# A conditioning projection weighed on VectorE and GpSimd instead of multiplied on TensorE, in a two-block fp32 kernel

## What is computed

```python
h = rms_norm(x, pre_ffn_norm)
u = causal_dwconv(h @ w_up, ffn_conv_w, ffn_conv_b)   # 3 taps, 2 x 2816 channels
gate, up = jnp.split(u, 2, axis=-1)
f = (jax.nn.silu(gate) * up) @ w_down
return x + rms_norm(f, post_ffn_norm)
```

```python
def ada_mod(cond, w, b):
    m = jax.nn.silu(cond) @ w + b
    return jnp.split(m, N_MOD, axis=-1)

sh1, sc1, g1, sh2, sc2, g2 = [m[:, None, :] for m in ada_mod(c, w_ada[l], b_ada[l])]
csh1, csc1, cg1, csh2, csc2, cg2 = ada_mod(c_ctx, w_ada[l], b_ada[l])
hc = modulate(rms_norm_2(h_ctx, norm1_g[l]), csh1, csc1)
hx = modulate(rms_norm_2(x, norm1_g[l]), sh1, sc1)
```

## Time and profile before

| | before |
|---|---|
| median of three runs | 1722.95 us |
| profiled execution, its own time | 1724.31 us |
| its span, from the first to the last instruction | 1722.5 us |
| TensorE busy, matmuls | 1638.2 us (95%) |
| TensorE weight loads | 1323.6 us (77%) |
| VectorE busy | 919.8 us (53%) |
| ScalarE busy | 661.0 us (38%) |
| GpSimd busy | 162.8 us (9%) |
| mean granted clock of TensorE | 0.983 |
| DMA | 180.13 MB, mean 105 GB/s |

### The profile page before, as it was taken

How to read it: one execution, slowest core, us unless ns; L and a number is a source line. 1 busy time by engine, 2 the same in 40 slices (tenths; PEclk the granted TensorE clock), 3 DMA queues, 4 the chain that set the end, 5 groups by cost and what they waited for, 6 DMA issues and landing times.

```text
span 1722.5 us, 21472 instructions
## 1 busy us (share of the span) xinstructions
PE 1638.2 (95%) x8319; PEld 1323.6 (77%) x8319; DVE 919.8 (53%) x1383; ACT 661.0 (38%) x1000; POOL 162.8 (9%) x174
## 2 busy tenths in 40 slices
PE   7989989899989899999999999999999799999998
PEld 6777768778868677777788778878777688888886
DVE  5657856774644555545534637865546533333334
ACT  5444465553323433333332532444444322232221
POOL 2011206210000100000000112251000000000000
PEclk9999999999999999999999999999999899999999
DMA  7243324221025366565342322222214133332222
GB/s 197 74 111 86 86 62 111 61 63 49 25 98 193 120 191 217 162 205 166 132 164 97 98 79 61 80 71 67 65 63 130 51 93 94 96 97 98 98 97 73
DMA packets 195687, 180.13 MB, mean 105 GB/s; under 512 B 6014, under 2 KB 175053, under 8 KB 192532
## 3 DMA queue, kind: packets, MB, share of 16 engines
q1 hardware_dynamic: 191888, 169.56, 32.5%
q10 hardware_dynamic: 2564, 8.00, 1.4%
q0 software_dynamic: 1152, 1.44, 0.4%
HBM read 174.63 MB, written 4.58 MB: 104 GB/s over the span
## 4 chain that ended last, share of the span: by engine, by line
PE 67%; DVE 4%; ACT 2%; issue 1%; POOL 0%; POOLq 0%; DVEq 0%; ACTq 0%
PE acc L623 11%; PE acc L624 10%; PE acc L625 10%; PE acc L654 6%; PE acc L656 6%; PE acc L655 6%; PE acc L1130 2%; PE acc L1132 2%; PE acc L1131 2%; PE acc L668 1%; PE acc L667 1%; PE acc L666 1%; PE acc L1077 1%; PE acc L1270 1%; PE acc L1254 1%
## 5 line engine op out<-in xcount | busy, mean ns | idle before, releaser
L1957 DVE TENSOR_TENSOR w_low<-w_raw,w_high 128x1024 fp32r<-128x1024 f32 x230 | 285.2, 1241 | 608.1 <-ACT w_high L1330 607.5
L623 PE MATMUL acc<-h_high,w_high 128*128 128x512 f32 x1216 | 488.0, 401 | 16.1 <-DVE arena L2066 4.9
L1330 ACT ACTIVATE w_high<-w_raw 128x1024 fp32r<-128x1024 f32 x224 | 237.1, 1058 | 633.0 <-PE acc L625 358.9
L624 PE MATMUL acc<-h_low,w_high 128*128 128x512 f32 x1216 | 477.3, 393 | 0.0
L625 PE MATMUL acc<-h_high,w_low 128*128 128x512 f32 x1216 | 477.1, 392 | 0.0
L623 PEld LDWEIGHTS acc<-h_high,w_high 128*128 128x128 f32 x1216 | 231.0, 190 | 94.4 <-issue 29.4
L625 PEld LDWEIGHTS acc<-h_high,w_low 128*128 128x128 f32 x1216 | 230.6, 190 | 49.6
L624 PEld LDWEIGHTS acc<-h_low,w_high 128*128 128x128 f32 x1216 | 230.9, 190 | 46.9 <-issue 1.2
L654 PE MATMUL acc<-w_high,act_high 128*128 128x512 f32 x496 | 194.2, 392 | 4.2 <-DVE arena L2642 1.5
L656 PE MATMUL acc<-w_high,act_low 128*128 128x512 f32 x496 | 193.5, 390 | 0.0
L655 PE MATMUL acc<-w_low,act_high 128*128 128x512 f32 x496 | 193.5, 390 | 0.0
(11 more groups left out here) (372 smaller groups left out, 1923.4 us busy)
## 6 DMA issues: line engine op xcount, KB each, us to landing
w_raw<-w_in SPq DMA_DIRECT2D x68, 512.0 KB, 3.9
w_raw<-w_mlp SPq DMA_DIRECT2D x64, 512.0 KB, 3.7
w_raw<-w_up SPq DMA_DIRECT2D x44, 512.0 KB, 3.9
early<-w_ada SPq DMA_DIRECT2D x22, 1024.0 KB, 6.0
w_raw<-w_out SPq DMA_DIRECT2D x24, 512.0 KB, 3.3
w_raw<-w_down SPq DMA_DIRECT2D x22, 512.0 KB, 3.2
w_raw<-w_branch_gate SPq DMA_DIRECT2D x16, 512.0 KB, 4.1
early<-decay_rows SPq DMA_DIRECT2D x4, 1024.0 KB, 9.6
```

The lines of the kernel that those rows point to most:

```text
L623: pe.matmul(out_, wh, xh, start=start, stop=False)
L624: pe.matmul(out_, wh, xl, start=False, stop=False)
L1330: f(WH[:, off % 2, :], RAW[:, off % 4, :], ACT.Copy).then_inc(sem("w_high"), 1)
L1957: tt(WL[:, off % 2, :], RAW[:, off % 4, :], WH[:, off % 2, :].bitcast(F32), ALU.subtract).then_inc(sem("w_low"), 1)
```

## The change

Only the sum over the 128 partitions stays on TensorE. VectorE multiplies each row of a slab by its conditioning value and adds it to an accumulator of 128 x 2048 (`weighed`, in two halves of 1024 columns, one after the taps of j=0 and one after the products), a slab per q by the table `ADA_DVE`. GpSimd does the same with whole slabs (`weigh_slabs`), a multiplication and an addition each: for slabs 0 to 7 with the context's column (these slabs are weighed by both engines), and for six more by `ADA_POOL`. For each third, `modulation` then multiplies the two accumulators by a column of ones in eight matmuls, after q=10, 14 and 20. The slabs have up to six places, and SyncE asks for slab m behind the weights of the q in `ADA_ASKED`, after whoever used the slab before in that place (`slab_used`). The up-projection alternates between banks 0, 1 and 4, 5, so that a block waits for the taps of four blocks earlier. The loops over q are written out on all engines, and the tile order of `down` follows the banks.

```diff
-SLABS = 24
+ADA_DVE = [[0], [1], [2], [3], [4], [5], [6], [7], [8], [10], [12], [13], [15], [], [], [18], [19], [20], [22], [23]]
+ADA_POOL = [9, 11, 14, 16, 17, 21]
+ADA_PLACE = [m % 4 if m < 18 else [4, 5, 0, 1, 4, 5][m - 18] for m in range(24)]
...
+ADA_ASKED = {1: [0, 1, 2, 3], 4: [4], 5: [5], 6: [6], 7: [7], 8: [8], 9: [9], 10: [10], 11: [11], 12: [12], 13: [13, 14],
+             14: [15], 15: [16, 17], 17: [18, 19], 18: [20], 19: [21, 22], 20: [23]}
...
+        def slab_used(eng, m):
+            if m in ada_order:
+                eng.wait_ge(sem("ada_mult"), 2 * ada_order.index(m) + 2)
+            if m < 8:
+                eng.wait_ge(sem("ada_pool"), m + 1)
+            elif m in ADA_POOL:
+                eng.wait_ge(sem("ada_pool"), 8 + ADA_POOL.index(m) + 1)
+        def ffn_bank(q, j):
+            return 4 * (q % 2) + j
...
-            sp.wait_ge(sem("d_ws"), 2 * NT - 2)
-            for m in range(2):
-                sp.dma_start(first_slab(m), ada_rows[m * P:(m + 1) * P, 0:2048]).then_inc(sem(f"ada_in{m}"), 16)
...
+                if m == 0:
+                    sp.wait_ge(sem("w_used"), UP_N + 2)
+                before = [n for n in range(m) if ADA_PLACE[n] == ADA_PLACE[m]]
+                if before:
+                    slab_used(sp, before[-1])
+                elif m > 3:
+                    sp.wait_ge(sem("mod_sum"), 2)
...
+            def modulation(third):
+                pe.wait_ge(sem("ada_mult"), [16, 26, 36][third])
+                pe.wait_ge(sem("ada_pool"), [8, 11, 14][third])
+                for i, at in enumerate((AD_[third], AG2_[third])):
+                    w = arena(at, 2048).rearrange("p (m g r) -> p m g r", g=4, r=32)
+                    for g in range(4):
+                        o = PS[32 * g:32 * g + 32, [6, 2, 3][third], :].rearrange("p (m r) -> p m r", r=32)
+                        m = pe.matmul(o, CDW[:, i if third == 0 else 0, :], w[:, :, g, :], start=i == 0, stop=i == 1)
+                m.then_inc(sem("mod_sum"), 1)
...
-            modulation(0)
-            modulation(1)
...
-                    pe.wait_ge(sem("ffn_step"), 5 * q + [2, 4][j])
-                    column_block(0, UP_N + 2 * q + j, j, HH, HL)
-                if q < 20:
-                    modulation(q + 2 if q < 11 else q + 3)
-                if q == 10:
-                    modulation(13)
-                if q == 19:
-                    modulation(23)
+                    if q > 1:
+                        pe.wait_ge(sem("ffn_step"), 5 * q - [3, 1][j])
+                    column_block(0, UP_N + 2 * q + j, ffn_bank(q, j), HH, HL)
+                if q in (10, 14, 20):
+                    modulation((10, 14, 20).index(q))
...
-            down(DN_N, DN_A, FF, lambda t, m: turn_x(0, 0) if t == NT - 1 else None, ffn_free, [2, 1, 3, 0])
+            down(DN_N, DN_A, FF, lambda t, m: turn_x(0, 0) if t == NT - 1 else None, ffn_free, [1, 3, 0, 2])
...
+            def weighed(m, part):
+                third, k = m // 8, m % 8
+                i = ada_order.index(m)
+                at = slice(part * 1024, part * 1024 + 1024)
+                acc, w = arena(AD_[third], 2048)[:, at], slab(m)[:, at]
+                slab_in(dve, m)
+                if i == 0 or ada_order[i - 1] // 8 < third:
+                    if third == 2:
+                        dve.wait_ge(sem("mod_sum"), 1)
+                    ts(acc, w, cond[:, k, 0:1], None, ALU.mult).then_inc(sem("ada_mult"), 1)
+                else:
+                    dve.wait_ge(sem("ada_mult"), 2 * i + part - 1)
+                    stt(acc, w, cond[:, k, 0:1], acc, ALU.mult, ALU.add).then_inc(sem("ada_mult"), 1)
...
+            def weigh_slabs():
+                def by(k, who):
+                    return cond[:, k, who:who + 1].to_broadcast([P, 2048])
+                pool.wait_ge(sem("n_low"), 12)
+                for m in [*range(8), *ADA_POOL]:
+                    third, who = m // 8, 1 if m < 8 else 0
+                    acc, w = arena(AG2_[third], 2048), slab(m)
+                    to = arena(M_, 2048) if m < 8 else w
+                    slab_in(pool, m)
+                    if m == 0 or m in (9, 16):
+                        if m == 16:
+                            pool.wait_ge(sem("mod_sum"), 1)
+                        pool.tensor_tensor(acc, w, by(m % 8, who), ALU.mult).then_inc(sem("ada_pool"), 1)
+                        pool.wait_ge(sem("ada_pool"), {0: 1, 9: 9, 16: 12}[m])
+                    else:
+                        step(pool.tensor_tensor(to, w, by(m % 8, who), ALU.mult))
+                        step(pool.tensor_tensor(acc, acc, to, ALU.add))
+                        pool.sem_inc(sem("ada_pool"), 1)
```

More of the change, by code:

```diff
@@ L54 @@
 END_N = M2_N + MF
-SLABS = 24
+ADA_DVE = [[0], [1], [2], [3], [4], [5], [6], [7], [8], [10], [12], [13], [15], [], [], [18], [19], [20], [22], [23]]
+ADA_POOL = [9, 11, 14, 16, 17, 21]
+ADA_PLACE = [m % 4 if m < 18 else [4, 5, 0, 1, 4, 5][m - 18] for m in range(24)]
+ADA_SEM = [place if place < 4 else place - 2 for place in ADA_PLACE]
+ADA_TURN = [sum(ADA_SEM[n] == ADA_SEM[m] for n in range(m)) for m in range(24)]
+ADA_ASKED = {1: [0, 1, 2, 3], 4: [4], 5: [5], 6: [6], 7: [7], 8: [8], 9: [9], 10: [10], 11: [11], 12: [12], 13: [13, 14],
+             14: [15], 15: [16, 17], 17: [18, 19], 18: [20], 19: [21, 22], 20: [23]}
 WO_A, DN_A, W2_A, M2_A = 0, 16, 16 + FF, 24 + FF
@@ L127 @@
 FF_ = 4096
-MR_ = M_
+MR_, MR2_, MRT_, MRT2_ = 15360, M_ + 5632, M_ + 4096, HT_
+AD_, AG2_ = (26624, M_ + 2048, 26624), (16384, M_, 16384)
 GR_, CS_ = 16384, 15360
@@ L348, in blocks, with slab_in @@
                     body(g, j)
-        def up_groups(eng, body):
-            with eng.Fori(0, FF // 8) as cg:
-                for i in range(8):
-                    body(8 * cg + i, i, cg)
-            for i in range(FF % 8):
-                body(FF // 8 * 8 + i, i, FF // 8)
-        def first_slab(m):
-            return arena(K0 * T + m * 2048, 2048)
-        def slab(m):
-            return E[:, (m % 2) * 2048:(m % 2 + 1) * 2048]
+        def slab(m):
+            place = ADA_PLACE[m]
+            if place < 2:
+                return E[:, place * 2048:(place + 1) * 2048]
+            return arena([FF_ + 14 * T, FF_ + 18 * T, XN_, XN_ + 2048][place - 2], 2048)
+        def slab_in(eng, m):
+            eng.wait_ge(sem(f"ada_in{ADA_SEM[m]}"), 16 * (ADA_TURN[m] + 1))
+        ada_order = [m for ms in ADA_DVE for m in ms]
+        def slab_used(eng, m):
[7 more added lines that the diff above has]
+            return 4 * (q % 2) + j
         def probs(u, e):
@@ L573, in _ @@
                     load(0, UP_N + 2 * q + j, w_up_v[:, :, q * P + j * (FF * P):(q + 1) * P + j * (FF * P)], P)
-                if 0 < q < 11:
-                    later_slab(q + 1)
-                if q == 11:
-                    later_slab(12)
-                if q > 10:
-                    later_slab(q + 2)
+                for m in ADA_ASKED.get(q, []):
+                    ask_slab(m)
                 if q == 2:
@@ L1069, in _ @@
             turn_mixed(2)
-            def modulation(m):
-                pe.wait_ge(sem(f"ada_in{m % 2}"), 16 * (m // 2 + 1))
-                w = (first_slab(m) if m < 2 else slab(m)).rearrange("p (m g r) -> p m g r", g=4, r=32)
-                for g in range(4):
-                    o = PS[32 * g:32 * g + 32, [6, 2, 3][m // 8], :].rearrange("p (m r) -> p m r", r=32)
-                    ins = pe.matmul(o, CDW[:, m % 8, :], w[:, :, g, :], start=m % 8 == 0, stop=m % 8 == 7)
-                ins.then_inc(sem("ada_used"), 1)
+            def modulation(third):
[7 more added lines that the diff above has]
+                m.then_inc(sem("mod_sum"), 1)
             pe.wait_ge(sem("cond"), 3)
-            pe.wait_ge(sem("x_res"), NT)
-            modulation(0)
-            modulation(1)
             turn_mixed(NT - 1)
@@ L2440, in ffn @@
                         w = PAR[:, 2, ds(q + (2 - lag) * 2 * FF + j * FF, 1)]
-                        stt(o, PS[:, j, 0:T - lag], w, o, ALU.mult, ALU.add).then_inc(sem("ffn_step"), 1)
+                        stt(o, PS[:, ffn_bank(q, j), 0:T - lag], w, o, ALU.mult, ALU.add).then_inc(sem("ffn_step"), 1)
+                    if j == 0 and q < len(ADA_DVE):
+                        for m in ADA_DVE[q]:
+                            weighed(m, 0)
                 dve.wait_ge(sem("ffn_gate"), q + 1)
@@ L2457, in modulated @@
                 dve.wait_ge(sem("mod_rows"), 2)
-                step(dve.transpose(MRT[:, 32:48, :].rearrange("p a b -> p (a b)"), MR[:, 2, :]))
-                step(tt(modT, MRT[:, :, 0:2], PAR[:, 4, 0:NADA].unsqueeze(2).to_broadcast([P, NADA, 2]), ALU.add))
+                step(dve.transpose(arena(MRT2_, 512), MR2))
+                for t in range(3):
+                    m = tt(modT[:, 16 * t:16 * t + 16, :], MRT[t][:, :, 0:2],
+                           PAR[:, 4, 16 * t:16 * t + 16].unsqueeze(2).to_broadcast([P, 16, 2]), ALU.add)
+                step(m)
```

(4 more changed lines are left out.)

82 lines of the change are left out of this document (45 added, 37 removed).

## The result

| | before | after the change |
|---|---|---|
| median of four runs each, on one chip | 1723.55 us | 1745.79 us (1741.39 to 1751.4) |
| ratio, 95% interval | | 1.0127 (1.0105 to 1.015) |
| profiled execution, its own time | 1724.31 us | 1744.17 us |
| its span | 1722.5 us | 1742.3 us |
| mean granted clock | 0.983 | 0.976 |

A forecast was written before the change was run, and what follows sets the result against it. TensorE was taken to bound the up-projection stage, busy 40.00 of 40.00 us. Terms of -19.5, +42.0 (waits) and +2.5 us (clock) gave +25: 1749 us profiled, 1748 against the median, range 1730 to 1768.

The forecast's parts named there:

- TensorE's part: Up-projection stage: slabs leaving TensorE save 25.7 us, three sums of eight matmuls cost 6.2 us; net -19.5 us.
- VectorE alone fits: Up-projection stage: VectorE's 6.4 us per q plus 2.6 us of weighing, 9.0 of 10.9 us, fits without GpSimd.
- GpSimd's prices: GpSimd's 128x2048 instructions: 3.65 us per multiplication, 4.7 us per addition, all 14 and 11 of them 103 us.
- The exclusion: VectorE and GpSimd instructions that each read two SBUF tensors exclude one another for full length; six such VectorE instructions per q.
- the term for the waits: TensorE in the stage loses 42 us to GpSimd work: 14.4 (slabs 0 to 3), 17.4 (4 to 7), 10.2 (six later).
- the one for the clock: TensorE's lower clock after idling, 1.7 us more per cold block, four or five gaps of 5 us or more: 2.5 us.
- The sign that I named: Profile of the stage: TensorE idle before column blocks, released by w_low, 40 us in sum, most in q=1 to 6.
- Bunched slabs: Slabs 4 to 7: a late VectorE bunches them in pairs of 16.7 us, costing 8.7 us twice, 17.4 us.
- rival 2: Blocking real but mostly absorbed: slabs arriving singly cost 1.9 us each, 32 down to some 20 us; 1723 to 1735; chance 0.06.
- the pause at its start: VectorE's own pause at the start of a run of GpSimd work, some 2 us, subtracted from that run's cost.
- Rival 1: GpSimd's long instructions do not hold VectorE, so only the -19.5 us is left: 1703 us; chance 0.11.
- Rival 3: SyncE stands behind slab_used, weights come late, slabs 4 to 11 cost a further 3 us each: above 1770; chance 0.05.

The follow-up runs named there:

- only writing: Changed kernel with GpSimd's weighing replaced by writing zeros, two 128x2048 instructions for each multiplication and each addition, same waits and counts: 1707.1 us, ratio 0.9903.
- the quiet kernel: Changed kernel with all weighing on GpSimd left out, its accumulators set to zero once and slabs only counted on: 1704.92 us, ratio 0.9882.

## Why the prediction was right

The sign and the mechanism are shown. The stage's lengths by GpSimd's instruction, with VectorE's work the same in all six rows:

| GpSimd's instruction | stage | TensorE idle | split, mean | GpSimd busy |
|---|---|---|---|---|
| 2048 columns | 288.7 us | 26.4 | 2068 ns | 111.2 us |
| 1024 columns | 263.8 | 12.2 | 1795 | 133.2 |
| 512 columns | 258.2 | 7.6 | 1698 | 158.1 |
| 256 columns | 265.5 | 12.4 | 1454 | 192.5 |
| only writing | 248.7 | 0 | 1224 | 91.4 |
| none | 248.3 | 0 | 1224 | 5.4 |

(The last two are those that leave out the weighing.) Point by point:

- **TensorE's part.** Forecast -19.5 us; measured -19.0 us in the stage with GpSimd quiet. The four banks, forecast at nothing, measured 0.9999. The order of the down-projection's tiles gave nothing either.
- **VectorE alone fits.** Forecast 9.0 of 10.9 us per q; the quiet kernel and the one in which VectorE does everything show no idle TensorE.
- **GpSimd's prices.** Multiplication forecast 3.65, measured 3.60 us; addition 4.7, measured 4.60 us. The slope from 512 and 1024 columns carried.
- **The exclusion.** Right, to the 1.07 us between GpSimd's end and the end of VectorE's. "Having passed one GpSimd instruction, VectorE does one of its own and waits for the next" is not exact: a product issued directly behind a short one slips in before GpSimd's next. Five waits per q, not six.
- **The size.** This is where the terms were mis-sized. I forecast 42 us of waits and 2.5 us for the clock, 44.5 in all; measured are 40.4 us, of which 26.4 idle and 14.0 in a TensorE that is busy longer (262.28 against 248.33 us) with the same 1104 matmuls. The clock accounts for most of the 14: by the timeline 70 matmuls of the stage follow each other at the lower level's distance, some 0.2 us too much each, against 15 with GpSimd quiet, which is about 11 us; the first matmuls behind the gaps make up another 1.8 us. "Four or five gaps of 5 us or more" were twelve of 0.3 to 3.4 us, and the lower level followed six of them, of 2.5 to 3.4 us. So the term for the waits was 16 us too high by the idle time, the one for the clock about 8 us too low (2.5 against about 11), and that the sum came within 4 us is in part luck. The two may be tied to each other, since VectorE catches up while TensorE runs slowly, but no run here separates them. The sign that I named, 40 us of idle TensorE, was 26.4. Taking length times the missing clock (in the first window less the 1.7 us of the entry) with the idle time, the groups come to 10.7 us for slabs 0 to 3 (forecast 14.4), 15.9 for 4 to 7 (17.4), and 12.7 for the later ones (10.2).
- **Bunched slabs.** Slabs 4 and 5 were weighed singly, from 635.45 and 653.80, and only 6 and 7 nearly together, from 674.50 and 684.12. That four such slabs still cost 15.9 us has two parts. Slab 4 alone came to a gap of 2.99 us and some 1.5 us of low clock, not the 1.9 us of rival 2; the pause at its start that I took off, some 2 us, was not there, for a weighing on VectorE waited at once, at 635.70. Slab 5 alone did cost what rival 2 has: two gaps of 0.28 and 1.70 us at full clock. The pair has the gaps of 2.51 and 3.39 us, each with low clock behind it.
- **Rival 1**, that long instructions don't hold VectorE, is refuted as a mechanism, yet its 1703 us is what the quiet kernel gives. **Rival 2** had the right idle time, 26 us against its 20 to 32, but not the clock. **Rival 3** showed only in the kernel with pieces of 256 columns, where GpSimd is slower.
- The forecast for the profiled execution, 1749, was 5 us high: 4.1 us from the sum of the losses, 0.5 from TensorE's part the other way, and 1.6 from what lies outside the stage.

That the exclusion is one of the ports to SBUF can't be told from these runs. They show that GpSimd's writing alone does not hold VectorE's subtractions, that VectorE's instructions with an operand in PSUM are not held (two taps from 674.87 take 1.53 us inside GpSimd's instruction from 674.50), and that the wait lasts to the end of an instruction. The trace agrees with the Trainium skill (SBUF — State Buffer, Who interferes with whom) in this.

## What to carry to other kernels

Before work is handed to GpSimd beside a VectorE that reads two SBUF operands, compare the length of one GpSimd instruction with the slack of the wait behind VectorE's. One instruction has to fit, and then the sum of the waits in a round has to fit as well: cutting into quarters, below the slack, turned +21 us of stage into -9 us here, but 9.8 us of loss stayed by the sum, and at 256 columns the pieces' own overhead made it worse again. If VectorE has the room, give it the work: with 250 instructions in the stage instead of 222 and no GpSimd beside it, it was busy for 39 us less. And an idle stretch of TensorE can cost more than its length: here 26.4 us of it came with 14 us of slower work, where gaps of up to 2.3 us (quarters and halves, 7.6 and 12.2 us in sum) came with only 2.3 and 3.3 us.
